# Two transformer blocks on one core: the last head pair of the first attention reordered around the output product

## The chip, the cores and the metric

The kernel runs on one core of a Trainium2 chip. The metric is the device time of one execution in microseconds, the median of several runs. The engines are named as the profile names them: PE is TensorE's matmul, PEld its weight load, DVE is VectorE, ACT is ScalarE, POOL is GpSimd, SP is SyncE, which here only issues loads.

## The reference, cut to what matters

The program computes two transformer blocks on 256 tokens of width 1024. The change touches the mixer of the first block, which is cut here to its core:

```python
q, k_c, v_c, k_s, v_s, k_w, v_w, gate_logits, u, v = split(h @ w_in)
# per query block of 128: three branches of attention
p_c = masked_softmax(q @ kc.T + bias)      # 15 compressed blocks
o = g0 * (p_c @ vc) + g1 * softmax(q @ k_s.T + bias) @ v_s + g2 * softmax(q @ k_w.T + bias) @ v_w
z_u = gelu(u)
z_v = layer_norm(gelu(v))
gm = z_u * (causal(w_s) @ z_v + b_s)
mixed = concatenate([o, gm], axis=-1)
out = mixed @ w_out                         # the output product
```

There are 8 heads of 64 and 2 query blocks of 128 rows. With 256 tokens all blocks of keys are selected and the window covers all, so both the selected and the window branch are full causal attention.

## The kernel before, in words

Everything is float32. A product is made of three matmuls: each operand is split into a high part (a copy rounded to fp32r, on ACT) and a low part (the rest, a subtraction on DVE), and high x high, high x low and low x high are added in PSUM.

**Weights** come through a ring of four buffers of 128 x 1024 in units. For each unit SP issues a load once both parts of the unit four places earlier are made (L563 waits, L564 issues; for the gate and up weights L597 and L599, two loads a unit). ACT then makes the high part (`split_to`, L869, about 1.05 us), once PE has used the unit that held the buffer, and DVE the low part (L1336, about 1.2 us). PE waits for the low part. How far ahead the splits go is written out by hand: `split_to(n)` stands at places in each engine's program, and each engine runs its program in the written order.

**The attention** of the first block runs over eight pairs n = 0..7 (two heads and one query block each; odd n has two key tiles). The stages of pair n are: logits on PE (`pair_logits`), maxima on DVE (`pair_max`, L1565), exponentials on ACT (`pair_exp`, L1069, two halves of two), the scaling by gate and sum on DVE (`pair_scale`, L1574 to L1579), 4 or 8 transposes on PE (`pair_transposes`, L2246), their copy from PSUM on ACT (`pair_pT`, L1080 for even n, L1083 and L1086 for odd n), the values product on PE (`pair_values`, L2261) and after every second pair a copy into `mix` on DVE (`pair_out`, L1585). PE's loop is L2340 to L2364. Between the parts of a pair PE fills in matmuls of other work (`fill`, L2199) up to n = 6; in n = 7 there is nothing left to fill in. `filled` says how many weight units this has used, and so what `split_to` asks for in the loop.

The compressed branch goes beside it: its probabilities `pc` are transposed (`block_transposes`, L2322, in n = 6), copied by ACT to `pcT` (L1130), and multiplied with the values (`block_values`, L2327): three head pairs in n = 7 into two banks that DVE adds to `mix` (L1621, L1622), and the fourth head pair straight into the accumulator after the loop. `read_u` (L1092) copies the projection u into `zu`; ACT applies the gelu to it (L1135) and DVE multiplies it into chunks 2 and 3 of `mix` (L1640).

**The output product** (`product(0, ...)`, L2026 to L2028) has eight units of weights: four for the first 512 output columns, four for the second. A unit is 12 matmuls. Its operand `mix` has four chunks, and the units take them in the order `MIX_ORDER` = 0, 2, 3, 1: chunk 0 is the first head pairs, 2 and 3 the gated part, 1 holds the last head pairs. Each chunk must first be split: ACT writes the high part (`mix_hi`, L1060), DVE the low part (`operand_lo`, L1336), and the product waits for it, chunk by chunk. After unit 0 PE runs `pair_values(7)`.

In ACT's program, the end of the stage is: copy `pcT` (n = 6), unit split, `read_u(1)`, exponentials of pair 7, `pair_pT(6)`, `mix_hi(0)`, gelu, and in the last turn of the loop (n = 8) `pair_pT(7)`; after the loop

```python
        mix_hi(2)
        mix_hi(3)
        split_to(s_wo.u0 + RING)
        mix_hi(1)
        boundary(0)
```

`boundary(0)` squares the first half of the product (L886), splits the remaining units of this product and the first units of the next (into `ff_hi`, held there), squares the second half (L897) and then normalizes, adds the residual, squares again and lets PE transpose the result (L2067) for the gate and up product.

Of the kernel before, what the change touches and what calls it, by code (L numbers as in the profile page):

```python
# [26 lines left out]
ACT = mybir.ActivationFunctionType  # L27
AX = mybir.AxisListType

P = 128  # L30
# [33 lines left out]
RING = 4  # L64
# [51 lines left out]
def _emit(nc, ctx, a, out):  # L116
# [384 lines left out]
    def chunk(c):  # L501
        return slice(CT * c, CT * c + CT)
# [36 lines left out]
    def filled(n, part):  # L539

        k_cmp = CMP_FIRST + sum(sum(p) for p in CMP_K[:n]) + (sum(CMP_K[n][:part]) if n < len(CMP_K) else 0)
        k_u = sum(sum(p) for m, p in U_K.items() if m < n) + (sum(U_K[n][:part]) if n in U_K else 0)
        return s_cmp.u0 + k_cmp // 4 + k_u // 4
# [302 lines left out]
    def _(act):  # L846
# [212 lines left out]
                act.wait_ge(mix_gm, c - 1)  # L1059
            act.activation(h_hi[:, chunk(c), :], mix[:, chunk(c), :], ACT.Copy).then_inc(h_hi_ready, 1)  # L1060

        def pair_exp(n):

            nk = P * (n % 2 + 1)
            for half in range(2):
                act.wait_ge(max_ready, 2 * n + half + 1)
                for br in range(2):
                    i = 2 * half + br
                    ins = act.activation(probs[:, n % 2, i * nk:(i + 1) * nk], pair_bank(n, half)[:, br, 0:nk], ACT.Exp,  # L1069
                                         bias=st1[:, n % 2, 0, i:i + 1], accum_out=st1[:, n % 2, 1, i:i + 1])  # L1070
            ins.then_inc(exp_ready, 1)

        def pair_pT(n):

# [14 lines left out]
        def read_u(b):  # L1089

            act.wait_ge(unit_used, s_u.u0 + 2 * b + 2)
            act.activation(zu[:, 2 * b:2 * b + 2, :], bank3[0], ACT.Copy).then_inc(act_read, 1)  # L1092

        for n in range(N_PAIR + 1):
            if n < N_PAIR:
                split_to(filled(n, 0) + 3)
                if n in (5, 7):
                    read_u((n - 5) // 2)
                pair_exp(n)
            if n >= 1:  # L1100
                pair_pT(n - 1)
            if n < N_PAIR:
                split_to(min(filled(n, 1) + 3, s_wo.u0 + RING))
            if n == 2:
                act.wait_ge(unit_used, s_cmp.u0 + 8)
                act.activation(hid_tok[:, :, :], bank3[0][0:2 * NCMP, :, :], ACT.Gelu_apprx_tanh
                               ).then_inc(act_read, 2)
            if n == 3:
                act.wait_ge(cmp_mm, 1)
                act.wait_ge(zero_ready, 2)  # L1110
                hid_T = bank[6][:, 0:8 * NCMP].rearrange("p (n m g j) -> p n m g j", n=2, m=2, g=G1)
                act.activation(hid_k[:, :, :, 0:NCMP], hid_T[:, 0, :, :, :], ACT.Copy)
                for m in range(2):
                    ins = act.activation(hid_v[:, m, :, :, 0:NCMP],
                                         hid_T[:, 1, m, :, :].unsqueeze(2).broadcast_to([P, G1, 4, NCMP]), ACT.Copy)
                ins.then_inc(cmp_act, 1)
            if n == 4:
                act.wait_ge(cmp_mm, 2)
                for half in range(2):
                    r64 = slice(64 * half, 64 * half + 64)  # L1120
                    ins = act.activation(kc_block[r64, :, half, :],
                                         bank[6][r64, P:P + 2 * NCP].rearrange("p (g j) -> p g j", g=G1), ACT.Copy)
                ins.then_inc(cmp_act, 1)
            if n == 5:
                act.wait_ge(cmp_dve, 2)
                act.activation(pc[:, :, :, 0:NCMP].rearrange("p t h j -> p (t h) j"),
                               pc[:, :, :, 0:NCMP].rearrange("p t h j -> p (t h) j"), ACT.Exp).then_inc(cmp_act, 1)
            if n == 6:
                act.wait_ge(cmp_mm, 4)
                act.activation(pcT[:, :, :], bank[6][:, 0:2 * P].rearrange("p (t q) -> p t q", t=TT), ACT.Copy  # L1130
                               ).then_inc(cmp_act, 1)
            if n == 7:
                mix_hi(0)
                act.wait_ge(act_read, s_u.act0 + 2)
                act.activation(zu[:, :, :], zu[:, :, :], ACT.Gelu_apprx_tanh).then_inc(zu_ready, 1)  # L1135
        mix_hi(2)
        mix_hi(3)
        split_to(s_wo.u0 + RING)
# [187 lines left out]
    def _(dve):  # L1326
# [17 lines left out]
        def split_to(u_end):  # L1344
            while done_units[0] < min(u_end, n_units):
                u = done_units[0]
                if u not in pool_lows:
                    if u - 1 in pool_lows:
                        dve.wait_ge(lo_ready, u)
                    split(None, 0, u)  # L1350
                done_units[0] += 1
# [6 lines left out]
        def operand_lo(c, base, src, turn=None):  # L1358

            dve.wait_ge(h_hi_ready, base + (c if turn is None else turn) + 1)  # L1360
            lo_of(h_lo[:, chunk(c), :], src[:, chunk(c), :], h_hi[:, chunk(c), :]).then_inc(h_lo_ready, 1)
# [243 lines left out]
        for n in range(N_PAIR + 1):  # L1605
            if n in (3, 5):
                pair_out((n - 3) // 2)
            if n == N_PAIR:
                break
            split_to(filled(n, 0) + 3)  # L1610
            if n == 6:
                dve.wait_ge(cmp_act, 3)
                link(dve.tensor_reduce(st_cmp[:, 1, :, :], p_cmp, AX.X, ALU.add))
                link(dve.reciprocal(st_cmp[:, 2, :, :], st_cmp[:, 1, :, :]))
                link(dve.tensor_tensor(st_cmp[:, 3, :, :], st_cmp[:, 2, :, :], gates[:, :, 0:24:3], ALU.mult))
                dve.tensor_tensor(p_cmp, p_cmp, over_slots(3), ALU.mult).then_inc(cmp_dve, 1)
            if n == 7:
                pair_out(2)
                dve.wait_ge(att_ready, 3)
                dve.wait_ge(cmp_mm, 5)  # L1620
                dve.tensor_tensor(mix[:, 0:2, :], mix[:, 0:2, :], bank3[2], ALU.add)  # L1621
                dve.tensor_tensor(mix[:, 2, :], mix[:, 2, :], bank3[3][:, 0, :], ALU.add).then_inc(att_ready, 1)  # L1622
            pair_scale(n)
            if n + 1 < N_PAIR:
                pair_max(n + 1)
            split_to(min(filled(n, 1) + 3, s_wo.u0 + RING))
            if n == 4:
                dve.wait_ge(cmp_act, 2)
                dve.wait_ge(zero_ready, 2)
                dve.tensor_tensor(vc_block[:, :, :], bank[6][:, 3 * DH:4 * DH].unsqueeze(1).broadcast_to([P, H1, DH]),  # L1630
                                  own_head[:, :].unsqueeze(2).broadcast_to([P, H1, DH]), ALU.mult).then_inc(cmp_dve, 1)
            if n == 5:
                dve.wait_ge(cmp_mm, 3)
                link(dve.tensor_reduce(st_cmp[:, 0, :, :], cmp_logits, AX.X, ALU.max, negate=True))
                dve.tensor_tensor(p_cmp, cmp_logits, over_slots(0), ALU.add).then_inc(cmp_dve, 1)
            if n == 7:
                operand_lo(0, H_MIX, mix, 0)
        dve.wait_ge(zu_ready, 1)
        for c in (2, 3):
            dve.tensor_tensor(mix[:, chunk(c), :], mix[:, chunk(c), :], zu[:, 2 * c - 4:2 * c - 2, :], ALU.mult  # L1640
                              ).then_inc(mix_gm, 1)
        operand_lo(2, H_MIX, mix, 1)
# [261 lines left out]
    def _(pe):  # L1904
# [433 lines left out]
        pe.wait_ge(toep_ready, H1)  # L2338
        pair_logits(0)
        for n in range(N_PAIR):  # L2340
            if n >= 1:
                pair_transposes(n - 1)
            if n == 5:
                block_logits()
            if n == 7:
                pe.wait_ge(cmp_act, 4)
                pe.wait_ge(exp_ready, 7)
                for hp in range(3):
                    ins = block_values(hp, 0, 2, bank3[2 + hp // 2][:, hp % 2, :], True)
                ins.then_inc(cmp_mm, 1)  # L2350
            fill(n, 0)
            if n == 4:
                block_keys_values()
            if n + 1 < N_PAIR:
                pair_logits(n + 1)
            fill(n, 1)
            if n == 3:
                hidden_transposes()
            if n == 6:
                block_transposes()  # L2360
            if n == 1:
                pe.wait_ge(sv_read, 2)
            if n >= 1:
                pair_values(n - 1)  # L2364
        block_values(3, 0, 1, bank[7][:, S:S + P], False)
        block_values(3, 1, 2, bank[7][:, S + P:2 * S], True)
        pair_transposes(N_PAIR - 1)
        pe.wait_ge(act_read, s_u.act0 + 2)
        product(0, h_hi, h_lo, MIX_ORDER, ready=lambda j: (h_lo_ready, H_MIX + j + 1),
                between={(0, 0): lambda: pair_values(N_PAIR - 1)})  # L2370
        last = gate_up(0, s_gu, 0)

        def shift_transpose():
# [301 lines left out]
```

## Time and profile before

| what | value |
|---|---|
| median of 3 runs | 960.68 us (960.01 to 961.21) |
| the profiled execution, its time | 960.92 us |
| its span in the profile | 959.2 us |
| PE busy, share of the span | 939.5 us, 98% |
| DVE, ACT, POOL busy | 661.7, 539.5, 234.9 us |
| attention of the first block and the output product | about 60 to 143 us from the span's start |

The profile is of one execution. The time is 1.7 us longer than the span (what lies around it). The stretch that the change touches is 112 to 132 us. A timeline row gives the start in us from the span's start, the duration in us, the engine, the line of the kernel, the operation, its output and inputs, its shape and how many there are; idle time ahead of it stands in brackets, with what ended it. PE's matmuls are pipelined, so a row can start before the one ahead of it ends, and their ends are modelled.

### The profile page before, as it was taken

The page shows a single profiled execution, that of the slowest core. Times are in us where ns is not written, and L with a number is a line of the kernel's source. Part 1 is how long each engine was busy: PE and PEld are TensorE (multiplying, and loading weights), DVE is VectorE, ACT ScalarE, POOL GpSimd, SP SyncE. Part 2 cuts the span into 40 slices and gives each one's busy share as a digit, 9 for nine tenths or more (in the row PEclk, how much of TensorE's full clock was granted, in tenths as well). Part 3 has the DMA queues.
Part 4 walks back from the last instruction along what each step waited for, and adds up shares of the span by engine and source line. Part 5 has one row for each costly group of instructions (what it writes and reads, how often), then busy time and mean ns, then how long its engine had stood idle before and what let it go on. Part 6 is the DMA issues. An engine that isn't in the chain of part 4 may idle for free.

```text
span 959.2 us, 15372 instructions
## 1 busy us (share of the span) xinstructions
PE 939.5 (98%) x5665; PEld 801.6 (84%) x5665; DVE 661.7 (69%) x1094; ACT 539.5 (56%) x952; POOL 234.9 (24%) x235
## 2 busy tenths in 40 slices
PE   8999999999999999999999999999999999999997
PEld 8987778888887898999878899996688878888786
DVE  5765677777786768965678766777966767755453
ACT  6677576444443667844455455567864654544443
POOL 5304102111123240399932144330200011000100
PEclk9999999999999999999999999999999999999999
DMA  9755347799988813750139766652344778666661
GB/s 282 235 163 177 112 154 248 223 282 282 290 276 258 257 44 111 204 170 23 46 103 342 214 176 176 175 162 71 117 159 154 241 241 247 194 187 190 194 219 67
DMA packets 131352, 179.00 MB, mean 187 GB/s; under 512 B 8124, under 2 KB 96910, under 8 KB 131280
## 3 DMA queue, kind: packets, MB, share of 16 engines
q1 hardware_dynamic: 120384, 144.53, 48.2%
q0 software_dynamic: 10304, 33.18, 11.6%
q8 instruction: 44, 0.72, 0.3%
q10 hardware_dynamic: 592, 0.34, 0.1%
q14 instruction: 28, 0.23, 0.1%
HBM read 176.90 MB, written 1.12 MB: 186 GB/s over the span
## 4 chain that ended last, share of the span: by engine, by line
PE 89%; ACT 4%; DVE 4%; issue 1%; DMA 1%; SPq 0%; DVEq 0%; ACTq 0%
PE bank L1947 18%; PE bank L2026 17%; PE bank L2028 17%; PE bank L2027 17%; PE bank L2199 1%; DMA w_raw<-in_w_in 1%; PE bank L2462 1%; PE bank L1978 1%; PE bank L2458 1%; PE bank L2485 1%; ACT w_hi L869 1%; DVE w_lo L1336 1%; PE bank L2393 1%; PE bank L2081 1%; PE bank L2622 1%
## 5 line engine op out<-in xcount | busy, mean ns | idle before, releaser
L1336 DVE TENSOR_TENSOR w_lo<-w_raw,w_hi 128x1024 fp32r<-128x1024 f32 (+1 forms) x239 | 284.0, 1211 | 85.2 <-ACT w_hi L869 84.9
L869 ACT ACTIVATE w_hi<-w_raw 128x1024 fp32r<-128x1024 f32 (+1 forms) x266 | 270.4, 1037 | 116.1 <-PE bank L2028 68.1
L2026 PE MATMUL bank<-w_hi,h_hi 128*128 128x512 f32 x448 | 179.0, 400 | 0.3 <-ACT work L1278 0.3
L2028 PE MATMUL bank<-w_hi,h_lo 128*128 128x512 f32 x448 | 174.8, 390 | 0.0
L2027 PE MATMUL bank<-w_lo,h_hi 128*128 128x512 f32 x448 | 174.4, 389 | 0.0
L1947 PE MATMUL bank<-h_hi,w_hi 128*128 128x256 f32 x432 | 124.4, 288 | 1.6 <-DVE h_lo L1489 1.3
L1947 PE MATMUL bank<-h_lo,w_hi 128*128 128x256 f32 x432 | 122.1, 283 | 0.0
L1947 PE MATMUL bank<-h_hi,w_lo 128*128 128x256 f32 x432 | 122.1, 283 | 0.0
L2026 PE MATMUL bank<-w_hi,ff_hi 128*128 128x512 f32 x272 | 107.6, 396 | 1.0 <-ACT work L1278 0.4
L2027 PE MATMUL bank<-w_lo,ff_hi 128*128 128x512 f32 x272 | 106.0, 390 | 0.0
L2028 PE MATMUL bank<-w_hi,ff_lo 128*128 128x512 f32 x272 | 106.0, 390 | 0.0
L2028 PEld LDWEIGHTS bank<-w_hi,h_lo 128*128 128x128 f32 x448 | 84.1, 188 | 17.9
L2026 PEld LDWEIGHTS bank<-w_hi,h_hi 128*128 128x128 f32 x448 | 84.2, 188 | 16.3 <-ACT work L1278 0.5
L2027 PEld LDWEIGHTS bank<-w_lo,h_hi 128*128 128x128 f32 x448 | 84.3, 188 | 15.7
L715 POOL TENSOR_TENSOR w_lo<-w_raw,w_hi 128x1024 fp32r<-128x1024 f32 x27 | 65.3, 2418 | 119.1 <-DVE w_lo L1336 95.6
L1947 PEld LDWEIGHTS bank<-h_hi,w_hi 128*128 128x128 f32 x432 | 82.7, 192 | 3.0 <-DVE w_lo L1336 1.7
L1947 PEld LDWEIGHTS bank<-h_lo,w_hi 128*128 128x128 f32 x432 | 82.8, 192 | 0.0
L1947 PEld LDWEIGHTS bank<-h_hi,w_lo 128*128 128x128 f32 x432 | 82.7, 191 | 0.0
L724 POOL DMA_DIRECT2D ada_raw<-in_ada_w x48 | 34.5, 719 | 188.3 <-DVE ada_acc L1453 175.6
L815 POOL TENSOR_SCALAR ff_hi<-pos_f,own_pos 128x256 fp32r<-128x256 f32 x64 | 65.0, 1031 | 4.3 <-PE bank L2463 4.0
L1453 DVE SCALAR_TENSOR_TENSOR ada_acc<-ada_raw,c_silu,ada_acc 128x512 f32<-128x512 f32 x84 | 63.0, 750 | 4.0 <-DVE ada_acc L1453 0.5
L2026 PEld LDWEIGHTS bank<-w_hi,ff_hi 128*128 128x128 f32 x272 | 51.1, 188 | 14.6 <-DVE w_lo L1336 2.5
(461 smaller groups left out, 1593.9 us busy)
## 6 DMA issues: line engine op xcount, KB each, us to landing
w_raw<-in_w_in SPq DMA_DIRECT2D x84, 512.0 KB, 3.8
ada_raw<-in_ada_w POOLq DMA_DIRECT2D x48, 512.0 KB, 6.2
w_raw<-in_w_gate_up SPq DMA_DIRECT2D x88, 256.0 KB, 5.3
w_raw<-in_w_ffn_in SPq DMA_DIRECT2D x88, 256.0 KB, 4.0
w_raw<-in_w_down SPq DMA_DIRECT2D x22, 512.0 KB, 6.6
w_raw<-in_w_ffn_out SPq DMA_DIRECT2D x22, 512.0 KB, 4.4
w_raw<-in_w_out SPq DMA_DIRECT2D x16, 512.0 KB, 3.5
w_raw<-in_w_o_ssd SPq DMA_DIRECT2D x16, 512.0 KB, 3.5
```

The costliest lines, as they stand in the source:

```text
L715: pool.tensor_tensor(low(u, n), w_raw[:, u % RING, 0:n], high(u, n).bitcast(F32), ALU.subtract).then_inc(lo_ready, 1)
L724: pool.dma_start(ada_raw[:, j, :].rearrange("p (k c) -> p k c", k=2), ada[:, 2 * j:2 * j + 2, 512 * MOD_CHUNKS[c]:512 * MOD_CHUNKS[c] + 51 ...
L815: ins = pool.tensor_scalar(reached[:, n % 2, c, :], pos_f[:, 0:S], own_pos[:, 2 * n + c:2 * n + c + 1], None, ALU.is_ge)
L869: act.activation(high(u, n), w_raw[:, u % RING, 0:n], ACT.Copy).then_inc(hi_ready, 1)
L1336: return dve.tensor_tensor(dst, src, hi.bitcast(F32), ALU.subtract)
L1453: ins = dve.scalar_tensor_tensor(acc, src, c_silu[:, k:k + 1], acc, ALU.mult, ALU.add)
L1947: ins = pe.matmul(out_b[:, s, :], w[:, kk, c], x[:, k0 + k, :], start=k == 0 and s == 0 and step == 0, stop=k == sum(st.ks) - 1 and s == 1 ...
L1978: ins = pe.matmul(out_b[:, t, 0:ncol], x[:, k, c], w[:, kk, :], start=first, stop=end and last and t == 1, skip_group_check=True)
L2026: pe.matmul(out, x_hi[:, k, x], hi, start=start, stop=False, skip_group_check=True)
L2027: pe.matmul(out, x_hi[:, k, x], lo, start=False, stop=False, skip_group_check=True)
L2028: return pe.matmul(out, x_lo[:, k, x], hi, start=False, stop=stop, skip_group_check=True)
L2081: ins = pe.transpose(bank[4 + b % 2][:, k * S + t * P:k * S + (t + 1) * P], ffv_tok[:, b % 2, t, k * P:(k + 1) * P], ident)
```

## The change

On PE the transposes of the last pair, which stood ahead of the output product, go between its first and second unit, and the last values product moves from behind the first unit to behind the second. The compressed values of the first three head pairs go ahead of the transposes of pair 6. On ACT the two halves of the last exponentials go before and after the `pcT` copy, ahead of `read_u(1)` and without a unit split ahead of them; that split and the next both stand where `split_to(s_wo.u0 + RING)` is, after `mix_hi(3)`. The gelu is made in two halves, each with its own signal. On DVE the low part of chunk 0 goes ahead of the scaling of the last pair, and the multiplication of each of chunks 2 and 3 waits for its half of the gelu. ACT's order from `pair_pT(7)` on stays as it is.

```diff
@@ ACT @@
-        def pair_exp(n):
+        def pair_exp(n, halves=(0, 1)):
...
-            for half in range(2):
+            for half in halves:
...
-            ins.then_inc(exp_ready, 1)
+            if halves[-1] == 1:
+                ins.then_inc(exp_ready, 1)
...
         for n in range(N_PAIR + 1):
-            if n < N_PAIR:
+            if n < N_PAIR - 1:
                 split_to(filled(n, 0) + 3)
-                if n in (5, 7):
-                    read_u((n - 5) // 2)
+                if n == 5:
+                    read_u(0)
                 pair_exp(n)
+            if n == N_PAIR - 1:
+                pair_exp(n, (0,))
+                act.wait_ge(cmp_mm, 4)
+                act.activation(pcT[:, :, :], bank[6][:, 0:2 * P].rearrange("p (t q) -> p t q", t=TT), ACT.Copy
+                               ).then_inc(cmp_act, 1)
+                pair_exp(n, (1,))
+                read_u(1)
             if n >= 1:
                 pair_pT(n - 1)
-            if n < N_PAIR:
+            if n < N_PAIR - 1:
                 split_to(min(filled(n, 1) + 3, s_wo.u0 + RING))
...
-            if n == 6:
-                act.wait_ge(cmp_mm, 4)
-                act.activation(pcT[:, :, :], bank[6][:, 0:2 * P].rearrange("p (t q) -> p t q", t=TT), ACT.Copy
-                               ).then_inc(cmp_act, 1)
             if n == 7:
                 mix_hi(0)
                 act.wait_ge(act_read, s_u.act0 + 2)
-                act.activation(zu[:, :, :], zu[:, :, :], ACT.Gelu_apprx_tanh).then_inc(zu_ready, 1)
+                for half in range(2):
+                    act.activation(zu[:, 2 * half:2 * half + 2, :], zu[:, 2 * half:2 * half + 2, :],
+                                   ACT.Gelu_apprx_tanh).then_inc(zu_ready, 1)
@@ DVE @@
-            split_to(filled(n, 0) + 3)
+            if n < N_PAIR - 1:
+                split_to(filled(n, 0) + 3)
...
                 dve.tensor_tensor(mix[:, 2, :], mix[:, 2, :], bank3[3][:, 0, :], ALU.add).then_inc(att_ready, 1)
+                operand_lo(0, H_MIX, mix, 0)
             pair_scale(n)
             if n + 1 < N_PAIR:
                 pair_max(n + 1)
-            split_to(min(filled(n, 1) + 3, s_wo.u0 + RING))
+                split_to(min(filled(n, 1) + 3, s_wo.u0 + RING))
...
-            if n == 7:
-                operand_lo(0, H_MIX, mix, 0)
-        dve.wait_ge(zu_ready, 1)
         for c in (2, 3):
+            dve.wait_ge(zu_ready, c - 1)
@@ PE @@
         for n in range(N_PAIR):
-            if n >= 1:
-                pair_transposes(n - 1)
-            if n == 5:
-                block_logits()
             if n == 7:
                 pe.wait_ge(cmp_act, 4)
                 pe.wait_ge(exp_ready, 7)
                 for hp in range(3):
                     ins = block_values(hp, 0, 2, bank3[2 + hp // 2][:, hp % 2, :], True)
                 ins.then_inc(cmp_mm, 1)
+            if n >= 1:
+                pair_transposes(n - 1)
+            if n == 5:
+                block_logits()
...
-        pair_transposes(N_PAIR - 1)
         pe.wait_ge(act_read, s_u.act0 + 2)
         product(0, h_hi, h_lo, MIX_ORDER, ready=lambda j: (h_lo_ready, H_MIX + j + 1),
-                between={(0, 0): lambda: pair_values(N_PAIR - 1)})
+                between={(0, 0): lambda: pair_transposes(N_PAIR - 1), (0, 1): lambda: pair_values(N_PAIR - 1)})
```

## Rows read from the trace of the kernel before

**Rows 1.** The page: busy time of each engine, and the chain by engine.

```profile
PE 939.5 (98%) x5665; PEld 801.6 (84%) x5665; DVE 661.7 (69%) x1094; ACT 539.5 (56%) x952; POOL 234.9 (24%) x235
...
PE 89%; ACT 4%; DVE 4%; issue 1%; DMA 1%; SPq 0%; DVEq 0%; ACTq 0%
```

**Rows 2.** Waits of PE over the whole span, the longest in total.

```profile
PE bank L2067 <- DVE rstd L1367: 2.4, 3, 0.9
```

**Rows 3.** Timeline of PE, 112 to 124 us.

```profile
113.12 1.09 PE L2261 MATMUL bank<-pT,v_tok 128*64 128x128 f32 x16
114.15 0.66 PE L2246 MATMUL bank<-mats,probs 128*128 128x128 f32 x4
114.65 1.46 PE L2327 MATMUL bank<-pcT,vc_block 128*128 128x256 f32 x6
117.41 0.66 PE L2261 MATMUL bank<-pT,v_tok 128*64 128x128 f32 x8 [1.31 <-ACT pT L1080]
118.00 0.71 PE L2327 MATMUL bank<-pcT,vc_block 128*128 128x128 f32 x4
118.83 1.09 PE L2246 MATMUL bank<-mats,probs 128*128 128x128 f32 x8
119.68 0.48 PE L2026 MATMUL bank<-w_hi,h_hi 128*128 128x512 f32 x1
...
122.61 1.09 PE L2261 MATMUL bank<-pT,v_tok 128*64 128x128 f32 x16
123.63 0.50 PE L2026 MATMUL bank<-w_hi,h_hi 128*128 128x512 f32 x1
```

**Rows 4.** Timeline of ACT, 113 to 122 us.

```profile
113.23 0.38 ACT L1130 ACTIVATE pcT<-bank 128x256 f32<-128x256 f32 x1 [3.21 <-PE bank L2322]
113.51 1.05 ACT L869 ACTIVATE w_hi<-w_raw 128x1024 fp32r<-128x1024 f32 x1
...
114.94 0.48 ACT L1069 ACTIVATE probs<-bank,st 128x256 f32<-128x256 f32 x1
...
116.74 0.62 ACT L1080 ACTIVATE pT<-bank 128x512 f32<-128x512 f32 x1
117.27 0.63 ACT L1060 ACTIVATE h_hi<-work 128x512 fp32r<-128x512 f32 x1
...
119.21 1.06 ACT L1135 ACTIVATE zu<-zu 128x1024 f32<-128x1024 f32 x1
...
120.65 0.59 ACT L1086 ACTIVATE pT<-bank 128x512 f32<-128x512 f32 x1
121.13 1.15 ACT L1060 ACTIVATE h_hi<-work 128x512 fp32r<-128x512 f32 x2
```

**Rows 5.** Timeline of DVE, 111 to 120 us.

```profile
111.39 1.29 DVE L1565 TENSOR_REDUCE st<-bank 128x2 f32<-128x512 f32 x2 [0.21 <-PE bank L2226]
114.59 1.23 DVE L1336 TENSOR_TENSOR w_lo<-w_raw,w_hi 128x1024 fp32r<-128x1024 f32 x1 [1.92 <-ACT w_hi L869]
...
116.21 0.69 DVE L1621 TENSOR_TENSOR work<-work,bank 128x512 f32<-128x512 f32 x1
116.82 0.41 DVE L1622 TENSOR_TENSOR work<-work,bank 128x256 f32<-128x256 f32 x1
...
117.55 1.23 DVE L1579 TENSOR_TENSOR probs<-probs,st 128x1024 f32<-128x1024 f32 x1
118.69 0.68 DVE L1336 TENSOR_TENSOR h_lo<-work,h_hi 128x512 fp32r<-128x512 f32 x1
```

**Rows 6.** One stretch: its length, busy time, then PEclk (the granted clock), DMA share, GB/s.

```profile
116.00:120.00 4.00, 2.57 (x22) 2.06 (x22) 3.25 (x7) 3.97 (x8) 0.00 (x0) 1.00 0.40 131
```

**Rows 7.** Timeline of ACT at 135 us, of SP at 129 us, and that stretch's loads to landing.

```profile
135.16 2.01 ACT L869 ACTIVATE ff_hi<-w_raw 128x1024 fp32r<-128x1024 f32 x2
...
129.14 0.88 SPq L599 DMA_DIRECT2D w_raw<-in_w_gate_up  x2
...
DMA to landing us min/median/max: 3.6/4.4/5.3
```

## The prediction, made before the changed kernel was run

> **What bounds the kernel now.** I read the page first. PE is busy for 98% of the span, and 89% of the chain that ended last is PE [rows 1]. So an edit is worth what it takes from or adds to PE's idle time, plus any matmul it adds; work on ACT or DVE counts only where PE waits for it. The list of waits comes next: PE's largest is for the normalization at the block boundaries, 2.4 us in three waits, none over 0.9 [rows 2]. The stage that is changed has one wait of its own that is longer than any of these: in PE's timeline PE stands still for 1.31 us before the values of pair 6, until ACT's copy of the transposes (L1080) is there [rows 3]. ACT's timeline shows why [rows 4]: ahead of that copy stand a weight split (113.51), the read of u and four exponentials of some 0.45 us each (114.94 to 116.74), though the transposes it copies began at 114.15 and took 0.66 [rows 3]. DVE has a split there too (114.59), ahead of the additions (116.21) that chunk 0 of the product's operand needs [rows 5]. A second wait is small: the fourth block values end at 118.00 + 0.71 = 118.71, the transposes of pair 7 start at 118.83, when DVE's scaling has ended (117.55 + 1.23) [rows 3, 5]. So all the idle time there is to win is 1.31 + 0.12 = 1.43 us.
>
> **The change, part by part.**
>
> *Up to unit 0.* pair_values(5) is unchanged; the next PE instruction starts at 114.15 [rows 3]. Now that is the block values (6 matmuls, 1.46 us): 115.6. Their `pcT` is there at 113.61 as before [rows 4], since the first half of the exponentials fits ahead of it: the first maximum is out at about 112.05, half of 1.29 after 111.39 [rows 5], and two exponentials are 0.9 us, so 112.95 against 113.23. The transposes of pair 6 start at about 115.5 and end at 116.2. ACT by then has done the second half (113.51 + 0.9) and the read of u (0.6), so it idles, and the copy runs from 116.2 to 116.85. PE starts pair_values(6) at 116.9, where it was 117.41: **0.5 us won**, and a wait of 0.7 stays where 1.31 was. On DVE the additions start at 115.65 instead of 116.21 and end 1.02 later, at 116.7. `mix_hi(0)` stands 0.53 behind the copy [rows 4]: 116.75 to 117.4. The low part of chunk 0 (0.68) ends at 118.1 instead of 119.37. PE ends the fourth block values at 116.9 + 0.59 + 0.71 = 118.2, so **unit 0 starts at about 118.15**, with no wait. It was 119.68, but behind the 0.85 us of transposes that now come later. The scaling of pair 7 moves behind that low part: three DVE operations, about 1.6 us, to 119.7. Its cover is unit 0.
>
> *Transposes between units 0 and 1.* A unit takes 2.93 us to the next start (119.68 to 122.61) and the 8 transposes 1.09 [rows 3]. So they start at 121.1 and end at 122.2. All their inputs are there at 119.7.
>
> *What unit 1 waits for.* It needs chunk 2 of the operand, so `mix_hi(2)` on ACT and the low part on DVE. The gelu, the table load ahead of it and the multiplications are early enough: the gelu starts 1.94 after `mix_hi(0)` (117.27 to 119.21) [rows 4], so at 118.7; both halves end by 119.9, the two multiplications by 121. But in ACT's program `pair_pT(7)`, in the loop's last turn, still stands ahead of `mix_hi(2)`, and it waits for the transposes, which now come after unit 0. Everything queued behind it on ACT stands still: `mix_hi(2)`, `mix_hi(3)`, two weight splits, `mix_hi(1)`. From the end of the transposes: second copy starts (122.2), `mix_hi(2)` 0.48 behind it (120.65 to 121.13), 0.63 long, to 123.3 [rows 4], low part 0.68, to 124.0 [rows 5], and PE at 124.05. So **PE waits 1.9 us before unit 1**, a wait that is not in the trace of before: there the copies ran beside unit 0, and chunk 2 had been split by about 122.5, a microsecond before PE wanted it at 123.63 [rows 3, 4]. The trace shows this order at work: the transposes ended at 119.92, yet the second copy started at 120.65, since the gelu (119.21 + 1.06) and the first copy stood ahead of it [rows 3, 4]. The Trainium skill, page "TensorE: Matmul & The Clock Gate", Part 1, says that ScalarE and VectorE are strictly first in, first out. By that rule nothing behind the copies can pass them, and the sum stands; with an ACT that reordered, the rival of the hidden copies below would hold.
>
> *After it.* Unit 1 to 127.0, pair_values(7) (1.02) to 128.0, unit 2. Before, unit 2 started 2.9 after 123.63, at 126.5. That is **1.5 us later**. By waits: 0.7 + 1.9 now, 1.43 before, 1.2 more; PE also changes twice more between long matmuls and short ones, about 0.1 each (0.48 for a first matmul where the others take 0.39). I take **1.4**, with 1.1 and 1.8 as ends.
>
> *The moved splits.* Weight units 2 and 3 of the product are now split together after `mix_hi(3)`, which starts at 123.2: ACT 123.7 to 125.7, DVE 1.23 each, to 125.9 and 127.1. Unit 2 needs the first at 128.0, unit 3 the second at 130.9: covered by 2 us. Chunk 1: copy, `mix_hi(1)` and low part end 1.8 after 128.0, at 129.8, also covered. Their cost falls on SP, whose loads wait for the low parts in order: the product's seventh load goes out at 126.0 instead of 115.9, its eighth at 127.2; at 3.6 to 5.3 us to landing [rows 7] they are there by 131.3 and 132.5, about when the units of PE that free their buffers are done (130.9 and 133.6). Then the gate and up loads: the second unit of them went out at 129.14 [rows 7], 5.4 us after the last values product. Now the way from there is copy, high part, two weight parts on ACT and DVE, 0.4 + 0.6 + 1.05 + 1.23 + 1.23 = 4.5: 132.5, or up to 133.4 with the old 5.4. It landed 3.6 to 5.3 us after issue [rows 7], so 136.1 to 138.7, the likely value 137.8. ACT wants it at 135.16 + 1.0 + 1.4 = 137.5, in the middle of its chain to the second squares. So **0.3 us** more, between 0 and 1.2; before, it had landed by 134.4, well ahead of the need.
>
> *Downstream.* From the end of the product's first half on, ACT's chain and PE's both follow that end, so the shift is passed on whole; the rest is PE after PE [rows 1].
>
> **Sum.** 1.4 + 0.3 = +1.7 us on the profiled execution's 960.92, so 962.6. That execution lies 0.24 above the median of 960.68, so the median should come out at **962.4**. Within 0.2% (1.9 us, about what a measurement of this kernel can tell from no change) means 958.8 to 962.6.
>
> **Rivals.**
>
> 1. *The hidden copies: not slower.* If ACT had chunk 2 split before the transposes end at 122.2, the 1.9 us wait would not exist and the edit would win what it is built to win: 0.7 of 1.43, less 0.2 for the changes between matmul kinds: 960.2. For it: chunk 2 can be multiplied by 120.4. Against it: the written order of ACT's program. It decides at the start of `mix_hi(2)`: before 121.5 for this rival, 122.7 for mine. 0.05.
> 2. *Loads too late.* The product's and the next product's loads now go out in a bunch, and the second gate and up unit lands at the slow end: 1.4 + 1.2 = 2.6, with 963.3. It decides if that unit lands after 138. 0.2.
> 3. *Absorbed at the boundary.* PE waits up to 0.9 us there for ACT and DVE [rows 2]; if their work ran less late than PE's, up to 0.8 of the 1.4 would vanish: 961.3. Against it: their chain starts at the end of the same product half. 0.12.
> 4. *The clock.* The granted clock is 1.00, the 2.4 GHz level, even in the stretch that holds the 1.31 us wait [rows 6]; the new wait is longer than any there. Should the clock fall to 1.2 GHz for one unit after it, 12 matmuls take 0.23 longer each: 2.7 more, 965.1. 0.03. The same page of the Trainium skill, in "Why this matters for your kernels", warns that idle gaps between bursts of matmuls send the clock back to half; by rows 6 a wait of 1.31 us did not.
>
> My own case keeps 0.6: 962.4, give or take 0.5.
>
> **How the numbers follow.** The low end takes in rival 3 and my case with 1.1 and no landing delay (961.8, less 0.5 for the runs' spread): 961.3. The high end takes in 1.8 + 1.2 = 3.0: 963.7. Slower by over 0.2% starts at 962.6: a third of my case, most of rival 2, rival 4: 0.37. Faster by over 0.2% would need more than the whole 1.43 us of idle time: 0.03. The rest, 0.6, is no change.
>
> **What would show it.** In the changed profile: values of pair 6 on PE at about 116.9 after a wait of 0.7 (right: the stage's first half is won); unit 0 at 118.15; transposes of pair 7 at 121.1; then PE's longest wait, 1.9 us, ended by DVE's low part, with ACT idle before L1083 for over a microsecond; unit 2 at about 128. The second gate and up unit's high part at 137.5 to 137.8. If unit 1 starts before 122.5, my main step is wrong and the time falls to rival 1. If the wait is there and the total is below 961, something downstream took up the delay, and PE's waits at L2067 must have shrunk by it.

## The result and the profile after

The changed kernel takes 963.68 us (median of 8 runs, 963.29 to 966.64) against 960.98 for the kernel before in the same set: a ratio of 1.003, 95% interval 1.0021 to 1.0039. It is slower by 2.7 us, 0.02 us inside the upper end of the range that was given, but clear of no change, where most of the chance had been put. The profiled execution took 964.4 us with a span of 962.7, 3.5 more than before.

The page's busy times and its chain by engine, to be read against [rows 1]:

```profile
PE 941.8 (98%) x5665; PEld 802.8 (83%) x5665; DVE 662.0 (69%) x1094; ACT 539.8 (56%) x953; POOL 235.0 (24%) x235
...
PE 88%; DVE 4%; ACT 4%; DMA 2%; issue 1%; SPq 0%; DVEq 0%; ACTq 0%
```

PE runs the same 5665 matmuls and is busy 2.3 us longer with them. No added wait can do that: some matmuls have become slower. The longest waits of PE [rows 2]:

```profile
PE bank L2073 <- DVE rstd L1373: 2.5, 3, 0.9
PE bank L2032 <- DVE h_lo L1342: 2.3, 2, 2.1
...
PE bank L2267 <- ACT pT L1081: 0.8, 1, 0.8
```

The 1.31 us before the values of pair 6 is down to 0.77, and a wait of 2.1 for a low part is new. PE's timeline through the stage, against [rows 3]:

```profile
112.64 0.38 PE L2328 MATMUL bank<-mats,pc 128*128 128x128 f32 x2
112.95 1.09 PE L2267 MATMUL bank<-pT,v_tok 128*64 128x128 f32 x16
113.97 1.56 PE L2333 MATMUL bank<-pcT,vc_block 128*128 128x256 f32 x6
115.37 0.60 PE L2252 MATMUL bank<-mats,probs 128*128 128x128 f32 x4
116.74 0.66 PE L2267 MATMUL bank<-pT,v_tok 128*64 128x128 f32 x8 [0.77 <-ACT pT L1081]
...
118.20 0.47 PE L2032 MATMUL bank<-w_hi,h_hi 128*128 128x512 f32 x1 [0.16 <-DVE h_lo L1342]
...
121.04 1.03 PE L2252 MATMUL bank<-mats,probs 128*128 128x128 f32 x8
124.21 0.47 PE L2032 MATMUL bank<-w_hi,h_hi 128*128 128x512 f32 x1 [2.13 <-DVE h_lo L1342]
...
124.98 0.40 PE L2032 MATMUL bank<-w_hi,h_hi 128*128 128x512 f32 x1
125.22 0.39 PE L2033 MATMUL bank<-w_lo,h_hi 128*128 128x512 f32 x1
125.44 0.49 PE L2034 MATMUL bank<-w_hi,h_lo 128*128 128x512 f32 x1
125.74 0.63 PE L2032 MATMUL bank<-w_hi,h_hi 128*128 128x512 f32 x1
126.16 0.63 PE L2033 MATMUL bank<-w_lo,h_hi 128*128 128x512 f32 x1
...
128.43 1.35 PE L2267 MATMUL bank<-pT,v_tok 128*64 128x128 f32 x16
129.71 0.50 PE L2032 MATMUL bank<-w_hi,h_hi 128*128 128x512 f32 x1
```

Up to 124.21 this is the forecast, row by row (116.9, 118.15, 121.1, 124.05 were given). From 125.4 on, a second thing shows: the starts of matmuls in unit 1 lie 0.42 apart (125.74, 126.16) where they lay 0.22 to 0.24 apart (124.98, 125.22, 125.44 in the same unit), and each is shown with 0.63 us instead of 0.39. Unit 1 takes 4.22 us to the values product behind it, against 2.93 for unit 0 before [rows 3], and the values product 1.28 instead of 1.02. The stretch's granted clock (the column before the DMA share) says what it is:

```profile
126.00:128.00 2.00, 2.00 (x6) 1.39 (x5) 1.20 (x2) 0.00 (x0) 0.00 (x0) 0.50 0.29 54
```

0.50 is the lower of TensorE's two levels, 1.2 GHz, where [rows 6] had 1.00. In ACT's timeline, against [rows 4], the forecast cause of the wait stands: idle 1.94 us until the transposes, then two copies, and only then the high parts of chunks 2 and 3.

```profile
121.74 0.60 ACT L1084 ACTIVATE pT<-bank 128x512 f32<-128x512 f32 x1 [1.94 <-PE bank L2252]
122.23 0.59 ACT L1087 ACTIVATE pT<-bank 128x512 f32<-128x512 f32 x1
122.71 1.15 ACT L1060 ACTIVATE h_hi<-work 128x512 fp32r<-128x512 f32 x2
...
138.54 2.09 ACT L869 ACTIVATE ff_hi<-w_raw 128x1024 fp32r<-128x1024 f32 x2
```

The last row holds the high parts of the first two gate and up units: ACT waits for no load ahead of them.

To compare profiles whose earlier parts differ by up to a microsecond, I measure from the start of the compressed transposes (L2322 before, the `mats,pc` row above; 112.82 before, 112.64 after) to the start of unit 2, and to the first transposes at the boundary (`rstd,mT`; 143.68 before, 147.14 after). The first is 13.66 before (unit 2 starts at 126.48) and 17.07 after, the second 30.86 and 34.50. So 3.4 us were lost at unit 2 and 3.6 at the boundary. From there to the end of the span it is 815.5 in both.

### The profile page after: what moved, and what is told of

The parts are those of the page before. It is cut to its first block, busy times and chain, and to the rows that moved or that the text cites. A ratio compares the mean times of both kernels' runs of the same rounds, so it can differ in the third digit from the quotient of the medians.

```text
span 962.7 us, 15373 instructions
## 1 busy us (share of the span) xinstructions
PE 941.8 (98%) x5665; PEld 802.8 (83%) x5665; DVE 662.0 (69%) x1094; ACT 539.8 (56%) x953; POOL 235.0 (24%) x235
## 4 chain that ended last, share of the span: by engine, by line
PE 88%; DVE 4%; ACT 4%; DMA 2%; issue 1%; SPq 0%; DVEq 0%; ACTq 0%
PE bank L1953 17%; PE bank L2032 17%; PE bank L2034 17%; PE bank L2033 17%; PE bank L2205 1%; PE bank L2467 1%; DMA w_raw<-in_w_in 1%; PE bank L1984 1%; PE bank L2463 1%; PE bank L2490 1%; DVE w_lo L1342 1%; PE bank L2398 1%; PE bank L2087 1%; ACT w_hi L869 1%; PE bank L2627 1%
```

## The experiments

Theory: ACT's written order makes the wait of 2.1 us (1.4 to 1.8 us net), the wait lets the clock fall (1.5 us), and the late loads cost the rest. Rivals: the slow matmuls come of something else that the change moved, or were a disturbance of one execution; something other than the order holds chunk 2.

**All profiles, the two lengths in us, and the runs**

| kernel | to unit 2 | to the boundary | lowest mean clock of 2 us, 118 to 134 us | median, before beside it | ratio, 95% interval |
|---|---|---|---|---|---|
| before | 13.66 | 30.86 | 1.00 | | |
| changed | 17.07 | 34.50 | 0.50 | 963.68, 960.98 | 1.0021 to 1.0039 |
| changed, again | 17.06 | 34.44 | 0.50 | 964.64, 961.00 | 1.0022 to 1.0047 |
| high parts first | 13.12 | 31.46 | 1.00 | 962.62, 961.00 | 1.0005 to 1.0023 |
| 12 idle matmuls | 15.76 | 33.39 | 1.00 | 963.94, 961.00 | 1.0015 to 1.0037 |
| transposes back | 16.35 | 33.55 | 0.50 | 963.21, 961.00 | 1.0010 to 1.0028 |
| stall alone, rest as before | 17.23 | 34.45 | 0.53 | 964.19, 961.22 | 1.0015 to 1.0037 |
| 9 idle matmuls | 15.52 | 33.19 | 1.00 | 963.48, 961.22 | 1.0016 to 1.0036 |
| high parts first, splits placed | 13.13 | 30.46 | 1.00 | 960.71, 961.22 | 0.9986 to 1.0004 |
| scaling early, splits placed | 12.75 | 29.94 | 1.00 | 960.72, 961.22 | 0.9989 to 1.0007 |
| exponentials alone | 13.28 | 30.77 | 1.00 | 961.39, 961.48 | 0.9987 to 1.0005 |
| 5 idle matmuls | 15.50 | 33.26 | 1.00 | 965.31, 961.48 | 1.0024 to 1.0055 |
| scaling early, again | 12.76 | 29.95 | 1.00 | 960.96, 961.48 | 0.9987 to 1.0008 |

**The changed kernel again.**

> The changed kernel once more, unchanged. The theory of the clock (the wait of 2.1 us before unit 1 lets the granted clock fall, and about 8 matmuls and the last values product then run at half speed) expects the same picture in this execution: matmul spacing of 0.43 instead of 0.23 us somewhere within 10 us of the wait, and 2.3 to 3.3 us more than before. The rival (a single disturbed execution was profiled) expects spacing of 0.23 throughout and +1.2 to +1.7 us.

The picture repeats: the wait is 2.13 again, matmuls lie 0.43 apart from 125.5 on, unit 2 starts at 17.06, and the median is 3.6 above before. The disturbance of one execution is out.

**High parts first.** On ACT, from the changed kernel:

```diff
+            if n == N_PAIR:
+                mix_hi(2)
+                mix_hi(3)
             if n >= 1:
                 pair_pT(n - 1)
...
-        mix_hi(2)
-        mix_hi(3)
         split_to(s_wo.u0 + RING)
```

> The changed kernel with mix_hi(2) and mix_hi(3) ahead of pair_pT(7) on ACT. If ACT's written order makes the wait, chunk 2's low part is made by about 121.5 us, PE starts unit 1 right behind the transposes at about 122.1 with no wait and the clock stays at 1.00. Waits of 0.8 and 0.2 us stay, against 1.4 before, less 0.2 for two more changes between kinds of matmul: 0 to 0.6 us faster than before, so about 960.7. The rival (something other than the order holds chunk 2) expects the wait to stay over 1 us and the time over 962.

```profile
120.93 1.03 PE L2253 MATMUL bank<-mats,probs 128*128 128x128 f32 x8
121.72 0.48 PE L2033 MATMUL bank<-w_hi,h_hi 128*128 128x512 f32 x1
...
143.99 2.02 PE L2074 MATMUL bank<-rstd,mT 128*128 128x128 f32 x16 [1.73 <-DVE rstd L1374]
```

Unit 1 starts right behind the transposes, with no wait and full clock. So the place of these two instructions in ACT's order is worth 3.95 us at unit 2 of the profile (17.07 to 13.12). The stage is then half a microsecond ahead of before, yet 0.6 behind at the boundary, where PE waits 1.73 instead of 0.71, and the median is 1.6 above before (962.62, where 960.7 was expected), a clear loss that I had not expected. ACT's timeline of this run names what is late:

```profile
135.10 1.06 ACT L869 ACTIVATE ff_hi<-w_raw 128x1024 fp32r<-128x1024 f32 x1 [0.67 <-DMA w_raw<-in_w_gate_up]
136.42 1.06 ACT L869 ACTIVATE ff_hi<-w_raw 128x1024 fp32r<-128x1024 f32 x1 [0.26 <-DMA w_raw<-in_w_gate_up]
```

**Idle matmuls in the wait.** Behind `pair_transposes(7)`, into a bank that nothing reads (12 times here, 9 and 5 in the other two); they compute nothing for the result:

```diff
+            for _ in range(12):
+                pe.matmul(bank[4][:, 0:P], ident, ident, start=True, stop=True)
```

> The changed kernel with 12 idle matmuls of 128 columns on PE right behind the last transposes, into a bank that nothing reads, so that PE works through most of the wait without doing anything for the result. Each takes about 0.13 us, 1.6 us in all, so unit 1 starts no later, at about 124.2. The theory of the clock expects spacing of 0.23 in unit 1 and the time 1.5 to 2.0 us below the changed kernel's, about 1.2 to 1.5 above before. The rival (the slow matmuls have another cause, or cost nothing in the end) expects no gain over the changed kernel.

Each took 0.217 us instead of the 0.13 I had assumed from the transposes (the trace shows 24 records for the 12), 2.6 in all, so they outlasted the wait by about 0.3 us and this run mixed two effects. The clock stayed at 1.00, and unit 2 started 1.3 earlier than in the changed kernel. Nine fit the wait:

> The changed kernel with 9 idle matmuls of 128 columns behind the last transposes, now at the 0.217 us that each was seen to take in the run with 12, so 1.95 us: PE works through nearly the whole wait of 2.1 and unit 1 starts no later than in the changed kernel. The theory of the clock expects 0.23 in unit 1 and unit 2 starting 1.5 us earlier, counted from the transposes of the compressed probabilities (17.0 us after them in the changed kernel, 15.5 here). The rival expects no difference.

```profile
120.47 1.04 PE L2252 MATMUL bank<-mats,probs 128*128 128x128 f32 x8
121.34 2.17 PE L2378 MATMUL bank<-mats 128*128 128x128 f32 x18
123.64 0.47 PE L2032 MATMUL bank<-w_hi,h_hi 128*128 128x512 f32 x1
...
126.57 1.09 PE L2267 MATMUL bank<-pT,v_tok 128*64 128x128 f32 x16
127.59 0.50 PE L2032 MATMUL bank<-w_hi,h_hi 128*128 128x512 f32 x1
```

Unit 1 starts at 11.57 from the compressed transposes, exactly where the changed kernel has it (124.21 - 112.64), and unit 2 at 15.52 instead of 17.07. **1.55 us is the price of the clock alone**, with the wait's length untouched. At the boundary 1.3 of it is left, since the loads come late again (below).

> The changed kernel with 5 idle matmuls behind the last transposes: 1.1 us of the 2.1 are worked through and a wait of about 1.0 us stays ahead of unit 1, shorter than the 1.3 us after which before kept its clock. If the length of the single wait is what counts, spacing of 0.23 in unit 1 and unit 2 at 15.5 us from the transposes of the compressed probabilities, as with 9. If any wait there brings the clock down, 17.0.

Half filled, with a wait of 1.01 us left, the clock stays at 1.00 too and unit 2 starts at 15.50. The median of this run (four runs) is no lower than the changed kernel's all the same; its own profile lost its time elsewhere: PE's waits for low parts of weights behind the boundary come to 1.7 us instead of 0.4, with loads of `w_down` on the chain, where the changed kernel's profile has none.

The medians don't show what the profiles show here. With 9, 12 and 5 idle matmuls they lie 2.26, 2.94 and 3.83 above before, the changed kernel's two 2.70 and 3.64, and the intervals overlap. The run with 12 was expected 1.2 to 1.5 above before, so that was a miss. What the clock costs is shown by the profiled executions; that idle matmuls make the kernel faster is not shown.

**The wait alone.** From the kernel before, one wait in the call of the product:

```diff
-        product(0, h_hi, h_lo, MIX_ORDER, ready=lambda j: (h_lo_ready, H_MIX + j + 1),
+        product(0, h_hi, h_lo, MIX_ORDER, ready=lambda j: (h_hi_ready, H_MIX + 4) if j == 1 else (h_lo_ready, H_MIX + j + 1),
```

> The kernel before, with nothing of the change; only, PE waits ahead of unit 1 of the output product until ACT has written the high part of chunk 1, about 1.9 us after PE is ready for unit 1. The theory of the clock (idle time of PE is what makes the granted clock fall, whatever else is edited) expects spacing of 0.43 us for some 7 matmuls after it, with the granted clock at 0.5 in a stretch: 1.9 for the wait and 1.5 for the clock, 3.4 us slower than before in the profile. The rival (the moved work of the change, not the wait, brings the clock down) expects 0.23 throughout and 1.9 us.

```profile
125.91 0.47 PE L2026 MATMUL bank<-w_hi,h_hi 128*128 128x512 f32 x1 [1.91 <-ACT h_hi L1060]
126.21 0.41 PE L2027 MATMUL bank<-w_lo,h_hi 128*128 128x512 f32 x1
126.44 0.61 PE L2028 MATMUL bank<-w_hi,h_lo 128*128 128x512 f32 x1
126.85 0.63 PE L2026 MATMUL bank<-w_hi,h_hi 128*128 128x512 f32 x1
```

Nothing of the change is in this kernel, PE waits 1.91 us and the clock falls the same way. Unit 2 starts at 130.32, so unit 1 took 4.41 us instead of 2.85 (123.63 to 126.48 before), 1.56 more. Unit 2 is 3.57 later than before (17.23 against 13.66), 1.91 for the wait and nearly all the rest for the slow unit, and the boundary 3.59. So in this profile PE's idle time brings the clock down with nothing moved. The rival of the moved work is out.

**Transposes back.** `pair_transposes(7)` ahead of the product and `pair_values(7)` behind unit 0 again, the rest as in the changed kernel.

> The changed kernel with only the last transposes and the last values product where they were before: transposes ahead of unit 0, values behind it. All else of the change stays. DVE scales pair 7 behind the low part of chunk 0, until 119.6, so PE waits about 1.5 us before these transposes, and unit 0 starts at about 120.7; before unit 1 there is no wait, since the copies run beside unit 0. Idle time 0.8 + 1.5 = 2.3 against 1.4 before: about 0.9 us slower than before, 961.9, with the clock at 1.00 if only a wait of about 2 us makes it fall; if 1.5 us does too, 1.9 more, 963.8.

The second of the two cases that were stated (the clock falls here too) came out in the profile; the median is 2.2 above before, where that case gave 2.8. PE waits 0.77 and then 1.61 us ahead of the last transposes, and these already run slowly:

```profile
116.46 0.66 PE L2267 MATMUL bank<-pT,v_tok 128*64 128x128 f32 x8 [0.77 <-ACT pT L1081]
...
119.38 1.93 PE L2252 MATMUL bank<-mats,probs 128*128 128x128 f32 x8 [1.61 <-DVE probs L1585]
```

1.93 instead of 1.09 us, a granted clock of 0.50 from 120 to 122, and a unit 0 of 3.84 instead of 2.93. Unit 2 is 2.7 later than before (16.35), and so is the boundary. So DVE's new order (the low part of chunk 0 ahead of the scaling) needs the moved transposes: by itself it costs a wait and the clock.

**Exponentials alone.** As the last, and DVE's order put back too.

> The first half of the change alone: exponentials of pair 7 early, splits late, compressed values ahead of the transposes of pair 6. The last transposes stand ahead of unit 0 again, the last values behind it, and DVE scales pair 7 ahead of the low part of chunk 0 as before. If this half saves what the prediction said, PE's wait ahead of the values of pair 6 is 0.8 instead of 1.3 and the clock stays at 1.00; unit 0 starts 0.5 us earlier, counted from the transposes of the compressed probabilities (6.4 against 6.86). At the boundary the late loads give back 0 to 0.6: 0.5 us faster to 0.1 slower than before. The rival (early exponentials cost as much elsewhere) expects no gain at unit 0.

```profile
118.20 1.09 PE L2253 MATMUL bank<-mats,probs 128*128 128x128 f32 x8 [0.22 <-DVE probs L1585]
119.05 0.48 PE L2033 MATMUL bank<-w_hi,h_hi 128*128 128x512 f32 x1
```

Unit 0 starts at 6.47 instead of 6.86: 0.4 won, where this half was priced at 0.5. At the boundary 0.1 of it is left, ACT waits 0.18 there for a load, and the time can't be told from before.

**The loads.** The high parts first, and besides, on ACT, a split behind `read_u(1)` (unit 2 of the product), and on both engines the split of its unit 4 ahead of chunk 1:

```diff
                 read_u(1)
+                split_to(s_wo.u0 + 3)
...
-        split_to(s_wo.u0 + RING)
+        split_to(s_wo.u0 + RING + 1)
         mix_hi(1)
```

> The kernel with mix_hi(2) and mix_hi(3) ahead of pair_pT(7), and besides ACT's split of the product's unit 2 behind read_u(1), where ACT idles, and the split of unit 4 on both engines ahead of chunk 1. In the run without these splits the stage was 0.9 us ahead of before at unit 2, and lost all of it at the boundary, where ACT waited 0.67 and 0.26 us for the gate and up loads. If those late loads are the cause, the first of them now goes out at about 126 instead of 129, both waits go, PE's wait at the boundary falls from 1.7 to 0.7, and the profile's span falls by 0.9 to about 958.5. The rival (the boundary takes the gain whatever the loads do) expects 959.5 again.

```profile
134.08 2.01 ACT L869 ACTIVATE ff_hi<-w_raw 128x1024 fp32r<-128x1024 f32 x2
...
142.60 2.02 PE L2075 MATMUL bank<-rstd,mT 128*128 128x128 f32 x16 [0.71 <-DVE rstd L1375]
```

Both high parts run on without a wait, the first gate and up load went out at 125.74 instead of 129.34, and PE's wait is 0.71 again. The stage is 1.0 us shorter than with the splits late (30.46 against 31.46) and 0.4 shorter than before, and the median fell from 1.6 above before to 0.5 below it. So the place of these splits is worth that microsecond. The run moves two of them at once: the change had put off the one of unit 2, the one of unit 4 stood late in the kernel before too, and which of the two counts was not separated. The span fell only to 959.0, by 0.5, since the parts outside the stage differ between executions.

**A version with the wait smaller still.** DVE scales pair 7 ahead of the compressed additions, PE does both sets of transposes ahead of unit 0, splits in idle time:

> A different order from the same parts: exponentials of pair 7 early as in the change, but the scaling of pair 7 ahead of the compressed additions on DVE, PE's transposes of pair 7 ahead of the fourth block values and unit 0, transposes of pair 6 first again, the last values product behind unit 0 as before, unit splits in ACT's and DVE's idle time. PE waits at most 0.5 us ahead of unit 0 and nowhere else in the stage, against 1.43 before; no second change between kinds of matmul. Expected: 0.9 us ahead at unit 2, kept at the boundary, span about 958.3; if the loads bind there, 959.2.

```profile
116.30 1.09 PE L2257 MATMUL bank<-mats,probs 128*128 128x128 f32 x8
117.23 0.61 PE L2338 MATMUL bank<-pcT,vc_block 128*128 128x128 f32 x4
118.44 0.47 PE L2037 MATMUL bank<-w_hi,h_hi 128*128 128x512 f32 x1 [0.60 <-DVE h_lo L1344]
```

One wait of 0.60 is left in the stage, and it is 0.92 us shorter than before (29.94). The interval still holds 1, so it was run again:

> The version with the scaling of pair 7 early once more, for its time against before. Its stage, from the transposes of the compressed probabilities to the first transposes of the boundary, was 0.9 us shorter than before (29.94 against 30.86). If that carries through, the median is 0.5 to 1 us below before; what the first set of rounds left open is whether an interval below 1 comes of it. Rival: another 0.9998, the gain lost after the boundary.

29.95 in the stage, 0.5 below before in the median, 0.9987 to 1.0008. The gain is there in both profiles and the medians lie on the right side in both sets, but no set of runs sets it apart from no change. In the second profile the rest of the span, from the boundary on, was longer by 1.3 us than in the first, again with loads of `w_down` on the chain. Whether these loads, which lie in a product that is short of them anyway, take such a gain on average stays open. This version beats the changed kernel; that it beats the one before is not shown.

**Does the clock fall in every execution?** The profiles above are of one execution each. The record also has the mean granted clock of every execution over its whole span. A fall that costs 1.55 us takes at least 1.55 / 962 = 0.0016 off this mean, so an execution that reads 0.999 or 1.000 had no such fall.

| kernel | executions at 0.999 or 1.000, mean time | at 0.998 or less, mean time |
|---|---|---|
| changed | 4, 963.49 | 4, 964.66 |
| changed, again | 1, 962.17 | 7, 965.04 |
| stall alone | 5, 963.30 | 4, 964.94 |
| transposes back | 3, 963.22 | 8, 962.88 |

So the clock does not fall in every execution: at least 5 of 16 executions of the changed kernel and 5 of 9 of the stall alone had no such fall. In these two kernels the executions without it are 1.2, 2.9 (a single one) and 1.6 us faster, about the price that the profiles gave; with the transposes back they are not faster. The right-hand column is no proof of a fall at this place, since 22 of the 79 executions of before that ran beside the experiments read 0.998 or less too. Part of that is the end of the span, where the granted clock in before's profile is 0.50 for the last microsecond. Nor does the length of the wait alone decide: the profile of the high parts first keeps 1.00 through and behind its wait of 1.73 us at the boundary, longer than the 1.61 (with 0.77 a few operations ahead of it) behind which the clock fell with the transposes back. What decides whether it falls stays open.

```profile
142.00:144.00 2.00, 0.27 (x3) 0.04 (x1) 1.63 (x5) 1.90 (x7) 0.00 (x0) 1.00 0.29 101
144.00:146.00 2.00, 2.00 (x17) 2.00 (x18) 1.83 (x4) 1.46 (x4) 0.00 (x0) 1.00 0.00 0
```

## Why the prediction was wrong, point by point

- **First half of the stage** ("0.5 us won, and a wait of 0.7 stays"): right. The waits went from 1.31 to 0.77, and the run of this half alone shows 0.4 at unit 0.
- **Transposes between units 0 and 1 make PE wait 1.9 us, by ACT's order**: right in mechanism and place; the wait was 2.13. The run with the high parts first shows that it is that order. The Trainium skill, page "TensorE: Matmul & The Clock Gate", Part 1, says of ScalarE that it is strictly first in, first out; here it idled 1.94 us, the last 1.5 of them with `mix_hi(2)`'s input multiplied (DVE's two multiplications start at 119.52 and take 1.29 together), so the trace agrees.
- **Net 1.4 at unit 2, ends 1.1 and 1.8**: too low. Without the clock's part, in the run with 5 idle matmuls, it is 15.50 - 13.66 = 1.84. The idle time came to 0.77 + 0.16 + 2.13 = 3.06 against 1.43, 1.6 more, where I had 1.2: each start after a low part on DVE lies 0.14 us behind its end, not 0.05, and I had left out the 0.16 ahead of unit 0.
- **Late loads 0.3, between 0 and 1.2**: the number came out in the changed kernel (3.64 - 3.41 = 0.2), but the cause that I gave is not in its profile: ACT waits for no load there, and its two high parts at 138.54 lie as far behind before's (135.16) as unit 2 does. Probably the slow matmuls gave the loads time. With full clock the step shows (with 9 idle matmuls ACT waits 0.23 for the second load), and it is 0.5 to 0.6 (30.86 against 33.26 and 33.19), and where the wait is gone too, 1.1 (the high parts first: 0.54 ahead at unit 2, 0.60 behind at the boundary).
- **The clock**: this is the step that failed. The sum put it at nothing. Rival 4 named the right event at the right place, and was given 0.03 because the clock had stood at 1.00 through 1.31 us of waiting [rows 6] and I let that stand for a wait half as long again. Its price was 2.7 for twelve matmuls; six or seven and parts of others ran slowly, and it cost 1.55 in the profile. The Trainium skill, page "TensorE: Matmul & The Clock Gate", section "Why this matters for your kernels", warns that idle gaps between bursts of matmuls send the clock back to half, but for gaps longer than any wait here. By that rule the clock would have stayed; with 1.91 and 2.13 us it fell in the profiles, and the measurement decides.
- **Downstream nothing**: right. From the boundary's first transposes to the end it is 815.5 us in both profiles.

Together: 1.84 for the waits and switches, 1.55 for the clock, 0.2 for the loads, 3.6 in the profiled stage, where 1.7 was forecast. The medians moved by 2.7 and 3.6, which fits a fall that only some executions have. That the first median lies inside the range is luck: the upper end was made of loads at their slowest, not of the clock. And without the fall the forecast was still short: the four executions at 0.999 average 2.5 above before, the profiles with 9 and 5 idle matmuls are 2.3 and 2.4 longer at the boundary, against the 1.7 of the sum, for the waits (1.84 instead of 1.4) and the loads (0.5 to 0.6 instead of 0.3).

## What to carry to other kernels

When work is moved on the consumer's engine, follow it on every engine that serves it: here PE's transposes were moved behind a unit, and the copy that waits for them stayed ahead of the copy that the next unit needs, on an engine that can't pass it by. A new wait of TensorE that is longer than those through which the trace of before shows the clock kept has to be priced with the clock, not only with its own length, and the price is paid in some executions and not in others, so look at the clock of each. Cheap matmuls in the gap, all of it or half, kept the clock in three profiles, but no gain of the median is shown for them; for the order without the wait, with the splits placed, it is (0.5 below before instead of 2.7 or 3.6 above). And a split or a load that is put off "behind" a critical step should be followed to the next stage: here the place of two splits decided over a microsecond there.

## What the runs showed of the hardware that I had not expected

- In the profiles, PE's granted clock fell to 0.50 after a wait of 1.91 us in otherwise full work (2.13 in the changed kernel, and 1.61 behind one of 0.77 a few operations earlier), and stayed at 1.00 where the waits were 1.31 and 0.12, 0.77 and 1.01, or 0.77 and 0.16. The length of the wait alone does not decide it: in the run with the high parts first PE waits 1.73 us at the boundary (up to 143.99) and the clock stays at 1.00, though it fell with the 1.61 of the transposes back. The fall shows 1.2 us after work resumes in the changed kernel (124.21, 125.44), 0.5 after it in the stall alone, and at once with the transposes back. It is not the same in every execution of one kernel: by their mean clock, at least 5 of 9 of the stall alone had no such fall.
- It came back by itself under work: the 16 matmuls of the values product at 128.43 took 1.28 us instead of 1.02, and unit 2 from 129.71 ran at 0.23 a matmul again. The price was 1.55 us in the changed kernel (17.07 against 15.52) and 1.56 in unit 1 of the stall alone.
- A matmul of 128 columns in plain f32 with `ident` as both operands shows two records and takes 0.217 us, not the 0.13 a transpose takes.
